# A decoder step whose projections are computed by seven block products in place of eight

## The reference

```python
z = rmsnorm(h, norm_g)
proj = einsum('btd,de->bte', z, w_in)             # 9 x 1024 columns
a_val, a_glu, a_gate, b_h, b_c, b_b, b_gate, m_a, m_b = split(proj)
u_a = a_val * sigmoid(a_glu)
c_a = layernorm(causal_dwconv31(u_a) + bias)      # per channel, 31 taps; samples use stored states
y_a = silu(c_a) * silu(a_gate)
y_b = b_b * causal_dwconv3(b_c * b_h) * silu(b_gate)
merged = sigmoid(m_a) * (y_a @ w_pa) + sigmoid(m_b) * (y_b @ w_pb)
y = rmsnorm(h + merged @ w_out, final_norm_g)
```

## Time and profile before

| | |
|---|---|
| median of 3 runs | 1141.34 us (1141.24 to 1142.58) |
| span of the profiled execution | 1139.5 us, 1.84 under that median |
| TensorE busy | 1122.1 us (98%) |
| VectorE busy | 629.0 us (55%) |
| ScalarE busy | 240.0 us (21%) |
| GpSimd busy | 147.3 us (13%) |
| moved by DMA | 75.34 MB, 21.2% of the 16 engines' span |
| mean granted TensorE clock | 0.999 of 2.4 GHz |

### The profile page before, as it was taken

The page is one execution under the profiler, slowest core; times in us unless marked ns, Lnnn a source line. Parts: engine busy times, 40 slices in busy tenths (PEclk is TensorE's granted clock), DMA queues, the critical chain, the costliest instruction groups (busy, mean ns, idle before and its releaser), DMA issues.

```text
span 1139.5 us, 17651 instructions
## 1 busy us (share of the span) xinstructions
PE 1122.1 (98%) x6868; PEld 1096.9 (96%) x6868; DVE 629.0 (55%) x890; ACT 240.0 (21%) x326; POOL 147.3 (13%) x70
## 2 busy tenths in 40 slices
PE   6999999999999999999999999999999999999997
PEld 5999999999999999999999999999999999998885
DVE  6568787877778877788785743002222223442223
ACT  7211111111110212111111322112323231122121
POOL 2000000000000000000031212121212123442220
PEclk9999999999999999999999999999999999999999
DMA  7211211102111121211112321131111113441221
...
DMA packets 101806, 75.34 MB, mean 66 GB/s; under 512 B 2735, under 2 KB 95279, under 8 KB 101764
## 3 DMA queue, kind: packets, MB, share of 16 engines
q1 hardware_dynamic: 101780, 74.97, 21.2%
...
## 4 chain that ended last, share of the span: by engine, by line
PE 97%; DVE 1%; ACT 1%; DMA 1%; issue 0%; SPq 0%
PE ps L1017 88%; PE ps L1192 8%; PE ps L1208 1%; DMA c<-in_x_prompt_dram 1%; DVE c L714 1%; ACT ua L462 0%; DVE z_lo L705 0%; PE spare L1135 0%; PE spare L1033 0%; PE spare L1090 0%; DVE t L714 0%; DVE t L991 0%; ACT sq L672 0%; ACT w_hi L442 0%; PE spare L1081 0%
## 5 line engine op out<-in xcount | busy, mean ns | idle before, releaser
L1017 PE MATMUL ps<-z_hi,w_hi 128*128 128x344 f32 (+2 forms) x1728 | 557.0, 322 | 0.9 <-DVE z_lo L705 0.9
L1017 PE MATMUL ps<-z_hi,w_lo 128*128 128x344 f32 (+2 forms) x1728 | 556.2, 322 | 0.0
L1017 PE MATMUL ps<-z_lo,w_hi 128*128 128x344 f32 (+2 forms) x1728 | 554.7, 321 | 0.0
L1017 PEld LDWEIGHTS ps<-z_hi,w_hi 128*128 128x128 f32 x1728 | 326.2, 189 | 2.2 <-DVE z_lo L705 1.6
L1017 PEld LDWEIGHTS ps<-z_lo,w_hi 128*128 128x128 f32 x1728 | 325.7, 189 | 0.2
L1017 PEld LDWEIGHTS ps<-z_hi,w_lo 128*128 128x128 f32 x1728 | 325.7, 189 | 0.0
L442 ACT ACTIVATE w_hi<-raw 128x1024 fp32r<-128x1024 f32 x82 | 86.8, 1059 | 580.6 <-PE ps L1017 565.5
L384 POOL TENSOR_TENSOR w_lo<-raw,w_hi 128x1024 fp32r<-128x1024 f32 x35 | 90.9, 2598 | 848.9 <-ACT w_hi L442 848.9
L765 DVE SCALAR_TENSOR_TENSOR sq<-ua,cst,sq 128x513 f32<-128x513 f32 x224 | 151.3, 747 | 0.0
L1017 PE MATMUL ps<-y_hi,w_hi 128*128 128x344 f32 x384 | 122.9, 320 | 0.0
L1017 PE MATMUL ps<-y_lo,w_hi 128*128 128x344 f32 x384 | 122.7, 319 | 0.0
(11 more groups left out here) (123 smaller groups left out, 667.6 us busy)
## 6 DMA issues: line engine op xcount, KB each, us to landing
raw<-in_w_in_dram SPq DMA_DIRECT2D x72, 512.0 KB, 3.6
t<-in_x_prompt_dram SPq DMA_DIRECT2D x9, 512.0 KB, 3.2
...
raw<-in_w_pb_dram SPq DMA_DIRECT2D x8, 512.0 KB, 4.0
raw<-in_w_pa_dram SPq DMA_DIRECT2D x8, 512.0 KB, 4.2
raw<-in_w_out_dram SPq DMA_DIRECT2D x8, 512.0 KB, 4.6
out_dram<-t SPq DMA_DIRECT2D x8, 512.0 KB, 2.6
```

The lines of the kernel that those rows point to most:

```text
L1017: last = nc.tensor.matmul(ps[s][:, ch, 0:width], w[:, s, k, :], x[:, k, lo_col:hi_col], start=(k == 0 and n == 0), stop=(k == K - 1 and n ...
```

## The change

Nearly every line of the kernel is rewritten; the output projection, the three-part float32 product and the formulas stay.

- **Seven products.** The work of a projection is cut into *units*: 256 output channels (two weight column blocks p and q of 128), 1024 input channels in two halves, and tokens in two halves of 524 (516 for w_pa and w_pb). This 2 x 2 x 2 block product is done by seven products of half size, with sums and differences of blocks. The sums of weights (u1 to u4) are made by four accumulating DMAs issued by GpSimd; those of tokens once for each of three operands (`x_sum`, VectorE). The products use seven *slots*, each with its own weight buffer `wop[:, s]` and token operand `xop[s]`; a product is 2 chunks x 4 k x 3 parts = 24 matmuls of 262 (258) columns. Products accumulate on one another in PSUM: slots 0, 2, 4, 6 in one pair of banks, 3 and 5 in a second, 1 alone. Between them the running sum is copied out (`first_product`, `third_product`, `fourth_product` on ScalarE) and combined by VectorE (`c11`, `c22`, `c12`); the fourth quarter is used straight from PSUM.
- **First unit.** Unit 0 is done with the plain eight products, of operands that need no sums.
- There are 44 units: three (glu+value, b_h+b_c, b_gate+b_b) for each of eight groups of channels, four a_gate units (unit 0 and one in each of groups 0 to 2), eight units of the two merge gates ("mix"), four of w_pb, four of w_pa.
- **Wide convolution.** The odd taps accumulate in `acc_b` and the sum-of-pairs taps in `acc_s`, two PSUM banks; the latter are now 15 taps 512 wide for 30 taps 256 wide. The even taps stay in SBUF (`acc_a`). ScalarE does the first taps. The 48 steps of a group are laid out over the next units by the tables SPREAD (groups 0 to 2) and TIGHT.
- **Low parts of weights.** All by GpSimd, six instructions a unit (five of 512 columns, one of 1024); the copies to `wop` by ScalarE.
- **Spills.** Branch A's convolution, both branches' y, all gates and branch B's result go to DRAM and come back. The layer norm reads c twice, over the units M to M+5 of the merge gates.

```diff
+SLOTS = 7
+SLOT_BANK = (0, 1, 0, 2, 0, 2, 0)
+FRESH = (0, 1, 3)
+W_READY = (1, 2, 3, 4, 4, 5, 6)
...
+        acc_b, acc_s = spare[0][:, 0:HALF], spare[1][:, 0:HALF]
...
+        SPREAD = {"short": (2, 9, 11, 13), "gate": (13, 20, 22, 23), "agate": (25, 33, 35, 36), "end": (38, 44, 46, 48)}
+        TIGHT = {"short": (3, 13, 15, 17), "gate": (17, 25, 27, 29), "end": (31, 42, 44, 48)}
...
+            def u1_sum(v):
+                pool.wait_ge(rb11_in, 16 * (v + 1))
+                pool.wait_ge(u13_in[v % 2], u13_at(v))
+                G.dma_start(u13[v % 2][:, 0, :], rb11, accum_op=ALU.add).then_inc(a1[v % 2], 16)
...
+            def w_lo(v, n):
+
+                pool.wait_ge(whi, w_at(v, n))
+                raw, s0, s1 = w_step(v, n)
+                G.tensor_tensor(wop[:, s0:s1, 1, :], raw, f(wop[:, s0:s1, 0, :]), ALU.subtract).then_inc(wlo, 1)
...
+            for u in range(1, NU):
+                v = u + 1
+                if u > 1:
+                    w_lo(u, 5)
+                if v < NU:
+                    w_lo(v, 0)
+                    u3_sum(v)
+                    w_lo(v, 1)
+                    u4_sum(v)
+                    w_lo(v, 2)
+                if v + 1 < NU:
+                    u1_sum(v + 1)
+                if v < NU:
+                    w_lo(v, 3)
+                if v + 1 < NU:
+                    u2_sum(v + 1)
+                if v < NU:
+                    w_lo(v, 4)
...
+            def conv_begin(j):
+
+                act.wait_ge(ua_ready, j + 1)
+                wait(act, conv_step, CONV_OPS * j)
+                A.activation(acc_a, ua[:, 0:2 * HALF + 1:2], ACT.Copy, scale=const(j, 0)).then_inc(conv_act, 1)
+                A.activation(acc_b, ua[:, 1:2 * HALF:2], ACT.Copy, scale=const(j, 1)).then_inc(conv_act, 1)
...
+                        ins = V.scalar_tensor_tensor(out=acc_s, in0=acc_u[:, i:i + HALF], scalar=tap_sum[:, j, i:i + 1],
+                                                     in1=acc_s if i else odd, op0=ALU.mult, op1=ALU.add)
...
+            def c11(u):
+                dve.wait_ge(prod, prod_at(u, 1))
+                dve.wait_ge(snap, snap_at(u, 0))
+                dst = half(p_buf(u), u, 0)
+                V.tensor_tensor(dst, psum_half(u, 1), dst, ALU.add).then_inc(ev, 1)
+
+            def c22(u):
+                dve.wait_ge(prod, prod_at(u, 4))
+                dve.wait_ge(snap, snap_at(u, 2))
+                dst = half(q_buf(u), u, 1)
+                V.tensor_tensor(dst, dst, psum_half(u, 4), ALU.subtract).then_inc(ev, 1)
+
+            def c12(u):
+                dve.wait_ge(prod, prod_at(u, 5))
+                dst = half(q_buf(u), u, 0)
+                V.tensor_tensor(dst, psum_half(u, 5), dst, ALU.subtract).then_inc(ev, 1)
+
+            def after_c11(u):
+                kind, i = UNITS[u]
+                if kind == "gate":
+                    dve.wait_ge(bsig_ready, 2 * i + 1)
+                    V.tensor_tensor(half(g2, u, 0), half(g2, u, 0), half(g1, u, 0), ALU.mult).then_inc(yb_step, 1)
...
+            def product(u, s, ch):
+                n = chunk_of(u)
+                out = bank(u, s)[:, ch, 0:n]
+                for k in range(KH):
+                    for m, (wp, xp) in enumerate(((0, 0), (0, 1), (1, 0))):
+                        last = T.matmul(out, wop[:, s, wp, P * k:P * (k + 1)], xop[s][:, xp, k, n * ch:n * (ch + 1)],
+                                        start=(s in FRESH and k == 0 and m == 0), stop=(k == KH - 1 and m == 2),
+                                        skip_group_check=(s not in FRESH))
+                return last
...
+            def slot_waits(u, s):
+                pe.wait_ge(wlo, w_at(u, W_READY[s] - 1))
+                p = phase_of(u)
+                if u == PHASE_START[p]:
+                    pe.wait_ge(xlo, x_at(p, s))
+                if s == 0:
+                    pe.wait_ge(*((gated0, 2) if u == 1 else (ev, snap_at(u - 1, 0))))
+                elif s == 1:
+                    pe.wait_ge(*((gated0, 3) if u == 1 else (ev, snap_at(u - 1, 2))))
+                elif s == 2:
+                    pe.wait_ge(snap, snap_at(u, 0))
+                elif s == 3:
+                    freed(u)
...
+                elif s == 4:
+                    pe.wait_ge(snap, snap_at(u, 1))
+                elif s == 5:
+                    pe.wait_ge(snap, snap_at(u, 2))
+                elif s == 6:
+                    pe.wait_ge(ev, snap_at(u, 1))
```

More of the change, by code:

```diff
@@ new lines, in x_at, with conv_index @@
+    def x_at(p, s):
+        return X0[s] if p == 0 else 8 + 7 * (p - 1) + s + 1
+    FINALS = 3 * PAIRS - 1
+    CONV_OPS = FINALS + 4
+    def conv_index(kind, i):
+        if kind in "ab":
+            return 3 * i - 2 + (kind == "b")
+        if kind == "sum":
+            return 0
+        if kind == "s":
+            return 3 * i + 3 if i < PAIRS - 1 else FINALS - 1
+        return FINALS + i
+    CONV_AT = {conv_index("sum", 0): ("sum", 0)}
+    for i in range(PAIRS):
+        for kind in "abs" if i else "s":
+            CONV_AT[conv_index(kind, i)] = (kind, i)
@@ L694, in _ @@
+            wo_high(2)
+            wo_high(3)
+            merged_high(0)
+            wo_high(4)
+            merged_high(1)
+            wo_high(5)
+            merged_high(2)
+            wo_high(6)
+            wo_high(7)
+            for t in range(TT):
+                if t + 3 <= TT:
+                    merged_high(t + 3)
+                final_norm(t)
+            final_norm(TT, DEC)
         @block.vector
@@ L1004, in _ @@
                 dve.wait_ge(half_added, h + 1)
-                V.tensor_tensor(half, ps[0][QUAD:QUAD + DEC, h, :], half, ALU.add).then_inc(h_ready, 1)
-            scale_rows(TT - 1, 0, DEC)
+                V.tensor_tensor(half_row, spare[h][QUAD:QUAD + DEC, :], half_row, ALU.add).then_inc(h_ready, 1)
+            scale_rows(TT, DEC)
         @block.tensor
         def _(pe):
-            def chunk(s, hi, lo, off, width, ch, k0=0, k1=K):
-                lo_col, hi_col = off + ch * width, off + (ch + 1) * width
-                for k in range(k0, k1):
-                    parts = ((w_hi, hi), (w_hi, lo), (w_lo, hi))
-                    for n, (w, x) in enumerate(parts):
-                        last = nc.tensor.matmul(ps[s][:, ch, 0:width], w[:, s, k, :], x[:, k, lo_col:hi_col],
-                                                start=(k == 0 and n == 0), stop=(k == K - 1 and n == 2))
-                if k1 == K:
-                    last.then_inc(chunk_done, 1)
@@ new lines, in plain_product @@
+            def plain_product(s, ch):
+                x, w, r = PLAIN[s]
+                out = first_bank(r)[:, ch, 0:CZ]
+                opens, closes = s in (0, 2, 4, 5), s in (1, 3, 6, 7)
+                for k in range(KH):
+                    for m, (wp, xp) in enumerate(((0, 0), (0, 1), (1, 0))):
+                        last = T.matmul(out, wop[:, w, wp, P * k:P * (k + 1)], x[:, xp, k, CZ * ch:CZ * (ch + 1)],
+                                        start=(opens and k == 0 and m == 0), stop=(closes and k == KH - 1 and m == 2))
+                return last
@@ new lines, in transpose_tails, with column_mean @@
+            def transpose_tails(j):
+                u = AT["gate", j] + 1
+                pe.wait_ge(tail_ready, 2 * j + 2)
+                freed(u)
+                T.transpose(bank(u, 3)[0:TAIL, 1, 0:P], tail_in, ident[:, :]).then_inc(tail_t, 1)
+            def column_mean(row, ch, left, done):
+                if ch == 2:
+                    pe.wait_ge(left, 1)
+                n = TOK // 3
+                T.matmul(spare[ch % 2][:, 0:n], ones[:, :], row[:, n * ch:n * (ch + 1)], start=True, stop=True)\
+                    .then_inc(done, 1)
@@ new lines, in out_half @@
+            def out_half(t, h):
+                if t < 3:
+                    pe.wait_ge(wo_lo, 4 * h + 4)
+                pe.wait_ge(mt_lo, t + 1)
+                if t >= 3:
+                    pe.wait_ge(h_ready, t - 2)
+                elif t == 2:
+                    pe.wait_ge(pa_step, 31)
+                for k in range(K):
+                    for m, (xp, wp) in enumerate(((0, 0), (0, 1), (1, 0))):
+                        last = T.matmul(pp[(t + 2) % 3][:, h, :], tile_op(t, xp)[:, k, :],
+                                        xop[2 * h + wp][:, k // KH, k % KH, 0:512],
+                                        start=(k == 0 and m == 0), stop=(k == K - 1 and m == 2))
+                return last
```

2219 lines of the change are left out of this document (1415 added, 804 removed).

## The result

The changed kernel takes 1204.97 us (median of 4 runs, 1199.34 to 1207.23) against 1141.43 before in the same sitting: a ratio of 1.0549, 95% interval 1.0523 to 1.0575. It is slower by 5.5%, where the forecast was 1084, 5% faster.

The account below looks back on a forecast made before the run. TensorE's matmuls were taken as the bound: 30 start + 909.9 products + 96.2 output + 6 transposes and means + 6.7 end = 1048.8 us, with stalls of 2 + 12 + 3 + 5 + 9 + 2 a 1081.8 span, 1084 us measured; range 1055 to 1135.

Parts of the forecast that it names:

- What bounds the kernel, the matmuls: Whole kernel: TensorE's matmuls bound it; product matmuls fall from 998 to 909.9 us, at 123.0 and 121.3 ns each.
- Step (d): Merge-gate (mix) units: 7.6 MB in 20.7 us each, 366 GB/s, makes them 5 us late; bounds 0 and 15.
- Step (g): Edits costed at nothing: ScalarE's copies, GpSimd's sum issues (1.2 us each), SP's queue, harmless until a spill is 20 us late.
- Step (c): Convolution groups: GpSimd's low parts delay VectorE 10.7 us a group; 12 us late in groups 3 to 7, 3 in 0 to 2.
- step (e): The two changes of operand: VectorE's seven passes of 2.2 us beside 4.6 us of its own cost 5 and 4 us.
- The start: Before and in unit 0: the first product needs five token tiles; 30 us of the start are idle.
- step (a): Unit 1: slots 3 and 5 wait for operands made in a row after the spill of unit 0's gates, 2 us.
- step (f): Output: its first tile needs the last merge, a high and a low part, uncovered, 2 us.
- (1): Rival: everything is hidden but half of step (a), step (e) and step (f); about 1057 us, chance 0.15.
- (2): Rival: GpSimd costs VectorE 12 to 19 us a group, or DMA its upper bound; 1110 to 1139 us, chance 0.2.
- (3): Rival: GpSimd costs VectorE its whole time, 26.7 us a group, groups 3 to 7 late 20.3 each; 1209 us, chance 0.08.
- (4): Rival: GpSimd's queue is the bound, 23.0 us a unit, 2.3 over in 43 units; 1183 us, chance 0.05.

Follow-up runs that it names:

- run 6: Changed kernel with the four weight sums of a unit as GpSimd additions instead of accumulating DMAs from unit 30 on: 1202.65 us, ratio 1.0533.
- run 7: Changed kernel with the layer norm's reads of c and of the gate cut to 64 of 1032 columns: 1186.90 us, ratio 1.0392.
- run 10: Changed kernel with the order changes of run 1, run 9, the first half of run 2 and the second of run 8: 1180.56 us, ratio 1.0351.
- run 1: Changed kernel with the merge-gate units' spills issued from ScalarE's queue instead of SP's: 1195.04 us, ratio 1.0463.
- run 2: Changed kernel with the 1 MB loads of the second and third operands later in SP's queue: 1200.19 us, ratio 1.0526.
- run 3: Changed kernel with GpSimd's low parts of the weights left out but for 16 columns from unit 2 on: 1163.86 us, ratio 1.0238.
- run 4: Changed kernel with the odd taps' accumulator moved from PSUM back to SBUF: 1233.04 us, ratio 1.0811.
- run 5: Changed kernel with the weight sums cut to 16 of 512 columns, still issued and waited for: 1180.46 us, ratio 1.0338.
- run 8: Changed kernel with unit 0's last sigmoid ahead of a weight copy, and unit 40's operand low part ahead of the merges: 1196.56 us, ratio 1.0479.
- run 12: Changed kernel with run 1, run 3, run 5, run 7 and the first half of run 2 together: 1113.43 us, ratio 0.9751.
- run 9: Changed kernel with two order changes at the start: VectorE's evacuations and ScalarE's first weight copy of unit 1 earlier: 1200.72 us, ratio 1.0526.
- run 14: run 10 plus, on ScalarE, unit 0's last sigmoid and the last operand's high part ahead of weight copies: 1180.21 us, ratio 1.0335.

## Why the prediction was wrong

**What bounds the kernel, the matmuls: right.** 121.8 ns at 262 columns for the forecast 123.0, 120.8 at 258 (20.29 us for 168) for 121.3. Had nothing else changed, the kernel would have been faster.

**Step (d), the DMA of the merge-gate units, failed first: 5 us, and an upper bound of 15, for 57 measured** (some 3 of them the column means, which the forecast has in its 6). I compared 366 GB/s wanted with 420 to 427 from the best slices of the start. But the earlier trace rows stood beside them: 49 GB/s at a DMA share of 0.17, which is 288 GB/s at a full share. The merge-gate units of the changed kernel move 240 at 0.83, 289 again. That the two agree is partly luck, since the quotient depends on the mix: it is 248 in units 2 to 12 (156 at 0.63) and 327 in the merge-gate units of run 6 (206 at 0.63), where the sums are gone from unit 30 on. The page of DMA queues has the sums lowest: 45.10 MB in 21.1% of the span, 178 GB/s, where the rest is 165.87 MB in 43.7%, 317 GB/s. 7.6 MB at 289 GB/s are 26.3 us, not 20.7. The eight units moved less than that, 6.6 MB each in the mean (240 GB/s over 220.8 us), and that at 289 is 22.9 us. So by my estimate some 20 of the 57 us are bytes. And 5 us of lateness took no account of a chain: store, read, passes, store (run 7), with VectorE in order between it and TensorE. How the 57 us divide between full engines and long single transfers stays open (run 6).

**Step (g), SP's queue harmless until a spill is 20 us late, failed.** It looked only at weight quarters held back by a spill. The spill held back by other transfers was the longest single wait, 16.5 us in unit 34. The same happened to a small load behind four large ones in unit 38, 12.2 us that the forecast has in no step. All orders together are worth 24.4 us (run 10); those of SP's queue gave 9.9 and 4.8 of it alone (runs 1 and 2), the others are of ScalarE's and VectorE's order.

**Step (c), GpSimd beside VectorE: the mechanism right, the place wrong.** Forecast 10.7 us a group, 8.5 of it where VectorE works; measured 7.3, and VectorE's own 48.8 for 49.5. The groups' lateness was right in sum (units 2 to 28: 21 for 15 and the transposes), but by luck: groups 0 to 2 lost 13.0 for 3, groups 3 to 7 7.9 for 12. In run 3 units 2 to 28 lost 4.5 in all, so GpSimd's work is behind most of both. The early groups, with the time of four units each, weren't as safe as I took them to be. That an accumulator in PSUM costs nothing was right too (747 and 748 ns), and run 4 shows that the groups live by it. What I didn't do was to apply the same exclusion to step (e).

**Step (e), the changes of operand: 9 us for 50 in units 36 to 43.** The changes themselves, units 36 and 40, lost 15.2 and 20.5; unit 38 is step (g)'s. In unit 36 the forecast's 15.4 + 4.6 us of work took VectorE 29.2, since passes of 2.2 us over 2064 columns became 2.78 and 2.99 in the mean, one of them 6.30. GpSimd's part is 15 (run 3), the weight sums' 8 (run 5); one order gave 6 in unit 40 (run 8); 29 were left with all of it gone (run 12).

**The start, step (a), step (f).** The first product came when forecast (25.24 us), but its second half of the tokens waited for an evacuation in VectorE's order until 34.5, and unit 1's first low part behind an operand that waited for a sum: +11. Unit 1 lost 12.1 for 2, and runs 8, 9 and 14 show that it is a chain: each wait removed came back one slot later. The output and end were 8 us longer than forecast; TensorE waited 6.60 us for the first tile's low part where step (f) had 2.

**A term that wasn't in the sum.** Behind many of the stalls the matmuls ran at the lower of the two clock levels: 27 us over the kernel. In the earlier trace rows TensorE never stopped, so no row there has its price. Here the product's line stood idle 105.4 us, so it is a quarter on top of the waits; in run 12 it is 16 on 34.9, nearly a half. It isn't in fixed proportion to a stall: a wait of 2.2 us in unit 3 has matmuls at 217 ns behind it, the same wait in unit 7 has them at 121.8.

**The rivals.** (1) and (2) ended on the wrong side. (3) is refuted: taps at 955 ns, under its 1.0 us, and groups 3 to 7 late by 1.6 us each, not 20.3. (4) is refuted: GpSimd is busy 12.8 us a unit there (192.07 over 15), and its sums' issues take 0.87 to 0.92 us where I took 1.2. The Trainium skill, "SBUF — State Buffer", section "Who interferes with whom", which I set beside (4), has VectorE starve GpSimd's descriptors in modes that few instructions here could use; the trace shows the sums landing in 4.6 us in the median against 3.4 for the weight quarters, and doesn't tell why. What the Trainium skill, "TensorE: Matmul & The Clock Gate", section "Back-to-back issue gap", gives was rightly left to the rows: its rule would make it 111.7 ns at 262 columns, 121.8 were measured. Slower, which came true, had 0.13, by mechanisms that weren't the ones: that (3)'s 1209 us stands 4 from the measured 1205 is luck.
